# Prompt attention scores as two products of rounded operands, with the high and low parts of queries and keys stacked over all 128 rows

## The reference

```python
# A) MoBA: block-sparse softmax attention with a position bias
s = jnp.einsum('bhqd,bhqnsd->bhqns', qc, kg).astype(jnp.float32) * scale
s = s - slopes[:, None, None, None] * dist
...
# B) stick-breaking attention
z = jnp.einsum('bhqd,bhld->bhql', qc, k).astype(jnp.float32) * scale
before = kpos[None, :] < pc[:, None]
log_keep = jnp.where(before, jax.nn.log_sigmoid(-z), 0.0)
```

## Time and profile before

| | us |
|---|---|
| median of 3 runs (lowest to highest) | 751.29 (750.43 to 753.71) |
| the profiled execution, its own time | 750.57 |
| its span in the profile | 748.6 |
| PE busy in the span | 698.0 (93%), 5542 products |
| DVE busy | 409.0 (55%) |
| ACT busy | 236.9 (32%) |
| POOL busy | 286.4 (38%) |

### The profile page before, as it was taken

How to read it: one execution, slowest core, us unless ns; L and a number is a source line. 1 busy time by engine, 2 the same in 40 slices (tenths; PEclk the granted TensorE clock), 3 DMA queues, 4 the chain that set the end, 5 groups by cost and what they waited for, 6 DMA issues and landing times.

```text
span 748.6 us, 13747 instructions
## 1 busy us (share of the span) xinstructions
PE 698.0 (93%) x5542; PEld 655.5 (88%) x5542; DVE 409.0 (55%) x661; ACT 236.9 (32%) x423; POOL 286.4 (38%) x183
## 2 busy tenths in 40 slices
PE   2999999999998698968989999999999999999993
PEld 1898998989987257967989999999999999999993
DVE  6424334454454437897984372653735627447247
ACT  5443444645456312234221221212212122122102
POOL 3852222322226205052843334444333333444407
PEclk9999999999999899989999999999999999999998
DMA  5243221212425763130132222222222222222303
GB/s 209 80 157 128 85 81 60 87 33 81 128 79 162 252 209 114 51 112 1 60 122 99 88 85 85 85 86 84 84 84 93 94 93 84 84 84 84 112 2 119
DMA packets 32814, 73.39 MB, mean 98 GB/s; under 512 B 3650, under 2 KB 18402, under 8 KB 32770
## 3 DMA queue, kind: packets, MB, share of 16 engines
q1 hardware_dynamic: 25634, 68.73, 26.9%
q10 hardware_dynamic: 6576, 3.38, 1.5%
q0 software_dynamic: 560, 0.66, 0.3%
HBM read 67.15 MB, written 5.60 MB: 97 GB/s over the span
## 4 chain that ended last, share of the span: by engine, by line
PE 80%; DVE 11%; DMA 4%; issue 2%; ACT 1%; SPq 1%; POOL 1%; ACTq 0%; DVEq 0%
PE acc L1359 67%; PE o_bank L1426 2%; PE s_bank L1400 2%; PE s_bank L1402 2%; DVE m_hi L1207 1%; DVE res L1136 1%; DVE hid L1205 1%; DMA k_t<-cache_k_a 1%; PE acc L1412 1%; DVE sq_sum L1158 1%; PE t_bank L1412 1%; DVE h_lo L1142 1%; PE acc L1442 1%; DMA v_b_sample<-kv_new 1%; DVE res L1131 1%
## 5 line engine op out<-in xcount | busy, mean ns | idle before, releaser
L524 POOL TENSOR_TENSOR w_lo<-w_raw,w_hi 128x1024 fp32r<-128x1024 f32 x90 | 217.6, 2419 | 375.4 <-ACT w_hi L632 375.4
L1359 PE MATMUL acc<-h_hi,w_hi 128*128 128x256 f32 (+1 forms) x864 | 265.7, 307 | 11.5 <-DVE h_lo L1142 7.2
L1359 PE MATMUL acc<-h_lo,w_hi 128*128 128x256 f32 (+1 forms) x864 | 250.8, 290 | 0.0
L1359 PE MATMUL acc<-h_hi,w_lo 128*128 128x256 f32 (+1 forms) x864 | 250.3, 290 | 0.0
L1359 PEld LDWEIGHTS acc<-h_hi,w_hi 128*128 128x128 f32 x864 | 164.8, 191 | 20.5 <-issue 10.3
L632 ACT ACTIVATE w_hi<-w_raw 128x1024 fp32r<-128x1024 f32 x90 | 94.9, 1059 | 246.4 <-PE acc L1359 231.6
L1359 PE MATMUL acc<-m_hi,w_hi 128*128 128x256 f32 (+1 forms) x576 | 166.6, 289 | 1.0 <-DVE res L1168 1.0
L1359 PEld LDWEIGHTS acc<-h_lo,w_hi 128*128 128x128 f32 x864 | 164.8, 191 | 2.6 <-issue 1.4
L1359 PE MATMUL acc<-m_hi,w_lo 128*128 128x256 f32 (+1 forms) x576 | 166.4, 289 | 0.0
L1359 PE MATMUL acc<-m_lo,w_hi 128*128 128x256 f32 (+1 forms) x576 | 166.3, 289 | 0.0
L1359 PEld LDWEIGHTS acc<-h_hi,w_lo 128*128 128x128 f32 x864 | 163.9, 190 | 0.0
(11 more groups left out here) (214 smaller groups left out, 745.8 us busy)
## 6 DMA issues: line engine op xcount, KB each, us to landing
w_raw<-weights SPq DMA_DIRECT2D x94, 512.0 KB, 3.2
k_t<-cache_k_a SPq DMA_DIRECT2D x16, 192.0 KB, 3.1
v_pg<-cache_v_a SPq DMA_DIRECT2D x16, 192.0 KB, 3.7
k_t<-cache_k_b SPq DMA_DIRECT2D x16, 192.0 KB, 5.0
v_pg<-cache_v_b SPq DMA_DIRECT2D x16, 192.0 KB, 3.7
xin<-x_prompt SPq DMA_DIRECT2D x4, 512.0 KB, 5.3
y_prompt<-y_n SPq DMA_DIRECT2D x8, 256.0 KB, 2.0
s_cst<-s_consts SPq DMA_DIRECT2D x1, 792.0 KB, 5.0
```

The costliest lines, as they stand in the source:

```text
L524: pool.tensor_tensor(w_lo[:, slot, :], w_raw[:, stage, :], w_hi[:, slot, :].bitcast(F32), ALU.subtract).then_inc(lo_done, 1)
L1359: mm = pe.matmul(out, w[:, slot, cols(k)], x[:, ks[k], halves(hf)], start=(k == 0 and pas == 0), stop=last)
```

## The change

The score product of each item becomes two products of rounded operands. The queries of a pair are copied into `q_st`, which has for each head two planes of 128 rows. In plane 0 the head's own 64 rows hold the high part of its queries and the other 64 rows the low part; in plane 1 they are swapped. The keys are copied into `k_st`, two planes (one for each head) with the high part in the head's own rows and the low part in the others. So the two products hold all four combinations of high and low. `k_st` borrows the rows 6 and 7 of `m_hi` and `m_lo`, which are written with other data after the last pair. `z_q` loses its zeroed planes: it is one plane, which each reader writes with one instruction over 128 rows, not two over 64. ACT writes the high parts and DVE the low parts, the queries in two parts of 256 columns.

```diff
-            for j in range(2):
-                pool.memset(z_q[j][:, :, :], 0.0).then_inc(zeroed, 1)
...
+            def stack_q_hi(i, part):
+
+                cols = Q_PARTS[part]
+                act.wait_ge(acc_act, 3 * i + 1)
+                act.wait_ge(acc_dve, 3 * i + 1)
+                if i:
+                    act.wait_ge(s_ready, 8 * (i - 1) + 4 * (part + 1))
+                for h in range(2):
+                    src = z_q[i % 2][OWN[h], NS + cols.start:NS + cols.stop]
+                    for order in range(2):
+                        act.activation(q_st[OWN[h ^ order], h, order, cols], src, ACT.Copy).then_inc(q_stack_hi, 1)
+
+            def stack_k_hi(i):
+
+                act.wait_ge(acc_act, 3 * i + 2)
+                act.wait_ge(acc_dve, 3 * i + 2)
+                for h in range(2):
+                    act.activation(k_st(i)[OWN[h], h, :], z_kv[i % 2][OWN[h], 0, PROMPT], ACT.Copy).then_inc(k_stack_hi, 1)
+
             for u in range(3):
                 read_half(u)
                 hi_unit(u + RING)
+                if u == 0:
+                    stack_q_hi(0, 0)
+                    stack_q_hi(0, 1)
+                elif u == 1:
+                    stack_k_hi(0)
...
+                    if i and s == 0:
+                        stack_q_hi(i, 1)
...
+                    if i + 1 < 2 * PAIRS and s == 4:
+                        stack_q_hi(i + 1, 0)
+                    if i + 1 < 2 * PAIRS and s == 6:
+                        stack_k_hi(i + 1)
...
-            for u in range(3):
-                read_half(u)
+            def stack_q_lo(i, part):
+
+                cols = Q_PARTS[part]
+                for h in range(2):
+                    dve.wait_ge(q_stack_hi, 8 * i + 4 * part + 2 * h + 1)
+                    z = z_q[i % 2][OWN[h], NS + cols.start:NS + cols.stop]
+                    hi = q_st[OWN[h], h, 0, cols].bitcast(F32)
+                    for order in range(2):
+                        dve.tensor_tensor(q_st[OWN[1 - (h ^ order)], h, order, cols], z, hi,
+                                          ALU.subtract).then_inc(q_stack_lo, 1)
...
+            read_half(0)
+            stack_q_lo(0, 0)
+            stack_q_lo(0, 1)
+            read_half(1)
+            stack_k_lo(0)
+            read_half(2)
...
-                q = z_q[i % 2][:, h, tile_cols(t)]
+                if s == 0:
+                    pe.wait_ge(k_stack_hi, 2 * (i + 1))
+                    pe.wait_ge(k_stack_lo, 2 * (i + 1))
+                if s in (0, 4):
+                    pe.wait_ge(q_stack_hi, 8 * i + 4 * (s // 4 + 1))
+                    pe.wait_ge(q_stack_lo, 8 * i + 4 * (s // 4 + 1))
                 out = s_bank[b]
+                q = q_st[:, h, :, P * t:P * (t + 1)]
+                k = k_st(i)[:, h, 0:L]
                 if i < PAIRS:
                     pe.matmul(out[:, 0:L], sid_r[:, 2 * i + h, :], dist_r[:, SEQ - L:SEQ], start=True, stop=False)
-                    pe.matmul(out[:, 0:L], q, z_kv[i % 2][:, 0, NS:NS + L], start=False, stop=True).then_inc(s_ready, 1)
+                    pe.matmul(out[:, 0:L], q[:, 0, :], k, start=False, stop=False)
+                    pe.matmul(out[:, 0:L], q[:, 1, :], k, start=False, stop=True).then_inc(s_ready, 1)
```

More of the change, by code:

```diff
@@ L168, in hybrid_layer @@
         v_tok = [sb(f"v_tok{j}", [P, QT, P], to=pr) for j in range(2)]
+        z_q1 = sb("z_q1", [P, T], to=pr)
         keep = sb("keep", [P, 2, SEQ], to=pr)
@@ L176, in hybrid_layer @@
         rinv = sb("rinv", [P, 2], to=pr)
-        z_q, z_kv = [], []
-        for j in range(2):
-            z_q.append(sb(f"z_q{j}", [P, 2, T], to=pr))
-            z_kv.append(sb(f"z_kv{j}", [P, 2, T], to=pr))
+        z_q0 = sb("z_q0", [P, T], to=pr)
+        z_q = [z_q0, z_q1]
+        z_kv = [sb(f"z_kv{j}", [P, 2, T], to=pr) for j in range(2)]
+        q_st = sb("q_st", [P, 2, 2, SEQ], F32R, to=pr)
         pr.close()
@@ L262, in hybrid_layer @@
         z_copied, q_copied = sem("z_copied"), sem("q_copied")
+        q_stack_hi, q_stack_lo = sem("q_stack_hi"), sem("q_stack_lo")
+        k_stack_hi, k_stack_lo = sem("k_stack_hi"), sem("k_stack_lo")
         kv_turned = sem("kv_turned")
@@ L343, in item, with k_st @@
             return i, s, s // 2, s % 2, P * (s // 2 + 1)
+        OWN = (slice(0, HD), slice(HD, P))
+        Q_PARTS = (slice(0, 2 * P), slice(2 * P, SEQ))
+        def k_st(i):
+            return (m_hi, m_lo)[i % 2][:, 6:8, PROMPT]
         def pt_bank(n):
@@ L550, in keep_samples @@
                 y, p = divmod(i, PAIRS)
+                if i == 0:
+                    pool.wait_ge(zeroed, 3)
                 pool.wait_ge(acc_act, 3 * i + 3)
@@ L678, in read_half @@
                     act.wait_ge(z_copied, i - 1)
+                    act.wait_ge(q_stack_lo, 8 * (i - 1))
+                if i >= 2 and j == 1:
+                    act.wait_ge(k_stack_lo, 2 * (i - 1))
                 if j == 0:
-                    for h in range(2):
-                        r = slice(HD * h, HD * (h + 1))
-                        op = act.activation(z_q[i % 2][r, h, halves(0)], acc[r, 0, 0:WIDE[0]], ACT.Copy, scale=SCALE)
-                    op.then_inc(acc_act, 1)
+                    act.activation(z_q[i % 2][:, halves(0)], src, ACT.Copy, scale=SCALE).then_inc(acc_act, 1)
                 else:
                     act.activation(z_kv[i % 2][:, j - 1, halves(0)], src, ACT.Copy).then_inc(acc_act, 1)
+            def stack_q_hi(i, part):
[13 more added lines that the diff above has]
+                    act.activation(k_st(i)[OWN[h], h, :], z_kv[i % 2][OWN[h], 0, PROMPT], ACT.Copy).then_inc(k_stack_hi, 1)
             for u in range(3):
@@ L1020, in _ @@
                                       ALU.subtract).then_inc(m_ready, 1)
+                if i and n < ITEMS and s == 0:
+                    stack_q_lo(i, 1)
                 if n < ITEMS and s in (2, 5, 7):
                     read_half(3 * (i + 1) + (2, 5, 7).index(s))
+                if i + 1 < 2 * PAIRS and s == 4:
+                    stack_q_lo(i + 1, 0)
+                if i + 1 < 2 * PAIRS and s == 6:
+                    stack_k_lo(i + 1)
             read_half(21)
```

20 lines of the change are left out of this document (12 added, 8 removed).

## The result

The changed kernel takes 747.05 us (median of 20 runs, 745.02 to 752.74) where the kernel before, run beside it, takes 751.75 (20 runs, 749.42 to 755.72). The ratio is 0.9939, 95% interval 0.9923 to 0.9954: 4.7 us faster, where 8.3 were forecast. The median lies just outside both stated ranges: 0.55 us above 746.5, and 0.05 us above the 747.0 of the wider one. The profiled execution took 748.88 us (before: 750.57), its span is 747.1.

A forecast was written before the change was run, and what follows sets the result against it. PE's own instruction stream was taken to bound the attention: 10.8 saved there, less 2.0 at the start and 0.5 at borders, gives 8.3 us, a median of 743.0 beside 751.29; range 739.5 to 746.5, 8 in 10 738.5 to 747.0.

The forecast's parts named there:

- PE's own work: Score products in the prompt attention: two rounded products for one full one save 1.80 us a pair, 10.8 over six.
- narrow items: Score items with L = 128: three narrow products at 0.11 us make 0.33, so nothing is saved.
- cheaper: Rival: narrow score products cost 0.06 us and the extras go, 12.9 us saved, 738.4 us; chance 0.10.
- the change does not do what it says: Rival: products of stacked operands run at half pace, only the waits stay, 753.8 us; chance 0.03.
- The borders: Between pairs, PE waits 0.1 to 0.2 us for turned probabilities: 0.5 us for all, bounds 0 to 1.2.
- the slower rival: PE waits for the stacks, at ten unhidden refills of the q stack: 25 us more, 768 us; chance 0.05.
- The start: Before the attention, PE waits 0.8 us for ACT's and 1.2 more for DVE's reading of unit 1: 2.0 us.
- the bound of 4.4: Upper bound of the wait at the start: DVE also loses POOL's unit of 42.18, 0.8 + 1.2 + 2.4 us.
- the 1.0 added: At the start, an estimated 1.0 us on DVE's subtractions for work POOL has in front without a gap.
- Behind the attention: Sample part, output projection and MLP: released by the attention's end, they move along whole, no change in length.

The follow-up runs named there:

- Experiment 4: The kernel before, with queries and keys rounded when read and two identical rounded products for the full one, no stacks: 741.45 us beside 751.47.
- Experiment 2: experiment 1 with the second part of each pair's queries stacked at s = 2, not s = 0: 750.66 us beside 751.47.
- experiment 1: The change, with only pair 0's first 256 query columns stacked at the start, on ACT before rounding unit 4; the rest at s = 0: 743.1 us beside 751.47.
- 9: The change measured again, on one chip with 10: 748.32 us beside 752.06 for the kernel before.
- 10: experiment 1 measured again, on one chip with 9: 743.51 us beside 752.06 for the kernel before.
- experiment 5: The change, with POOL waiting at the head of the MLP until DVE has written the first group's low parts: 744.9 us beside 751.49.
- 7: experiment 1, with POOL waiting at the head of the MLP until DVE has written the first group's low parts: 739.69 us beside 751.49.
- 3: The change without the second of each item's two products, all stacking kept: 742.98 us beside 751.47 for the kernel before.
- 6: The kernel before, with POOL waiting at the head of the MLP until DVE has written the first group's low parts: 749.62 us beside 751.49.
- experiment 8: The change, with POOL waiting for DVE's eight start subtractions before weight unit 4: 747.16 us beside 751.49 for the kernel before.

## Why the prediction was off by half

**PE's own work, 10.8 us: right.** Experiment 4 has it alone with 10.6 us in the trace; the products cost 0.12, 0.18 and 0.23 us; narrow items save nothing, since 0.06 + 0.11 + 0.11 and the 0.06 behind them make 0.34 where 0.33 was forecast; a pair is 1.6 to 1.8 us shorter, 1.80 forecast. The rival "cheaper" is out, and so is "the change does not do what it says".

**The borders, 0.5 us: right.** It is 0.3 us, well inside the bounds of 0 to 1.2 and along the path that was worked out: 0.12 and 0.15 us at the first two borders and next to nothing at the other three. The refills of `q_st`, which the slower rival rested on, make PE wait nowhere in the change. In the steady part none of its 40 subtractions met a POOL unit (420 ns in the mean). Experiment 2 shows how near that was.

**The start, 2.0 us: the step that failed.** It is 3.6 to 5.6 us in the five traces with that start, 4.8 in the mean; as differences of medians it is 4.0 (change against experiment 1), 4.8 (9 against 10) and 5.2 (5 against 7). These differences leave out that experiment 1 pays 0.7 us for the copies that it moved (165.6 against 164.9 us above). The mechanism was the one forecast; the term was mis-sized, in three parts. First, DVE's eight subtractions lost the second POOL unit as well, which I had only in the bound of 4.4. I had let DVE finish at 42.5, or 43.4 with the 1.0 added, with POOL's second unit starting at 42.18: that is already too late, and I took it for a miss. By the rows after, with one loss they would have ended at 37.35 + 8 x 0.45 + 2.07 = 43.0, and POOL's unit began at 41.84. The second part I had left out altogether: after the waits PE ran at half clock in three of the five traces, which made 24 products of 3.46 us last 4.8 to 5.0. The third is small: I took the start of ACT's rounding from one row, and it depends on when the raw weights land. It lay 1.74 (experiment 5), 2.17 (3), 2.37 (the change) and 2.78 us (9) behind DVE's reading of unit 0, and PE's wait for ACT was 0.6, 1.0, 1.2 and 1.6 us, where 0.8 was forecast from a trace with 1.90. With the measured terms the sum is 10.6 - 4.8 - 0.3 = 5.5 us, where 4.7 were measured (3.5 to 5.8 by the interval).

**Behind the attention, 0: right for experiment 4, in doubt for the kernels with stacks.** The text said the prediction would be wrong if that stretch changed its length by over 1 us, and in the profiled executions it did: the attention ends 6.4 us earlier (the projection product behind the last scores starts at 213.93 us, before at 220.35) and the span is only 1.5 us shorter. Of the 4.9 us given back, 3.6 are the longer class of the tail, some 2 for the relu and 1.5 for the clock, and 1.3 lie between the attention and the MLP, which differs more than that within one kernel. But that is one execution. If every timed run fell in that class, POOL's wait would save about 6 us; between the medians it saves 2.2 in the change, 3.4 in experiment 1 and 1.9 in the kernel before, where 2 is what the shorter class would give. So the medians put the cost of the tail to the kernels with stacks at something between nothing and 1.5 us, and their own error is about as large. Experiment 1 fits that: by its trace the attention gains 175.3 - 165.6 = 9.7 us, 8.4 and 8.5 (751.47 - 743.10, 752.06 - 743.51) were measured, with intervals of 6.9 to 12.2 and 6.5 to 10.2 us on the ratios, and 9.9 (7 against 6) once POOL's wait has made all tails alike.

**What stays open.** Why POOL's units at the head of the MLP run without a gap more often in the kernels with stacks; how often they do in runs that are not profiled; and why the clock falls at 47 us in one execution of the change and not in another. That PE's idleness has a part in it is likely: at the start the clock stayed at 1.00 in all seven traces without a wait there, and at the head of the MLP experiments 5, 6 and 7 took the wait away and it stayed at 1.00. Each of these is one execution.

## What to carry to other kernels

A run of short two-input subtractions on DVE need not lose to POOL only once: here it lost to every POOL subtraction that started before the run had ended, and each loss lengthened the run and brought the next one under it. So price such a run by iterating, and if its end falls within an estimate's error of the next POOL instruction, take the loss. Look for time in which the engine stands idle, as ACT does here ahead of the rounding that sets POOL going, put there only what is needed first, and put what another engine waits for ahead of the rest; here that was worth about as much as the whole measured gain. Judge a small give-back by many runs: a single profile here put 3.6 us on a place which the medians put at 1.5 or less. And when PE waits, look at its clock behind the wait as well: the wait may cost more than its length.

## What the runs showed of the hardware that I had not expected

A DVE subtraction of 0.42 us took 2.49 and 2.50 us when POOL had begun 0.36 and 0.38 us before it, and eight of them took 7.81, 7.78, 8.02, 8.68 and 9.10 us in five traces of the same order; with POOL held back 4.92 and 4.77, of which the first one took 1.76 (experiment 8) behind a unit that POOL had begun before. A cast with one input met the same: 2.35 and 2.36 us beside POOL at 288 columns, 0.29 us alone at 256.

TensorE's granted clock fell to 0.50 behind idle stretches of 1.6 and 1.8, 1.0 and 2.0, and 0.6 and 3.1 us, and stayed at 1.00 behind 1.2 and 1.8 us; the same kernel did the one in one execution and the other in another. At the head of the MLP it fell to between 0.50 and 0.60 behind each of the seven waits of 4.6 to 4.8 us. Such a wait is 2.0 to 2.2 us longer than that of the kernel before, and the tail behind it 3.5 to 4.9 us.
